# Five elementwise products per turn, on VectorE instead of GpSimd, in a two-layer retention and short-conv mixer

## The chip, the cores and the metric

The kernel runs on one core of a Trainium2 chip. The metric is the device time of one execution in microseconds (us), less is better. Three runs of the kernel before gave 1888.89, 1891.98 and 1894.93 us; their median, 1891.98, is the time before.

## What is computed

Two mixer layers over 256 tokens of width 2048, in f32. Cut to what matters here:

```python
mod = silu(c) @ w_ada + b_ada                    # shift, scale, gate
h = rmsnorm(x, norm_pre) * (1 + scale) + shift
z = h @ w_in                                     # 2048 -> 14336 columns
gb, gcin, u, g_c, q, k, v, g_r = split(z)
y_conv = gb * causal_conv3(gcin * u, conv_w)     # gcin * u: the conv gate product
y_conv = y_conv * silu(g_c)                      # gb * ...: the output gate
q, k = rope(q), rope(k) * DK ** -0.5             # t1*cos - t2*sin, t1*sin + t2*cos
y_ret = head_groupnorm(retention(q, k, v), gn_gain) * silu(g_r)
o = concat(y_conv, y_ret) @ w_out
x = x + gate * rmsnorm(o, norm_post)
```

## The kernel before, in words

**Tiling.** Activations lie transposed, channels on the 128 partitions and the 256 tokens in the free dimension. A layer is four *turns* (`TURNS`), each for two retention heads and a quarter of the conv channels. A turn goes through seven blocks of 512 weight columns in the order q/k, v, conv gate input (GC), u (UU), output gate of the conv (GB), g (GG), g_r (GR). A block is four *chunks* of 512 rows of `w_in` (1 MB each), so a turn has 28 chunks; chunk w of a turn belongs to block w // 4. After the turns come four output blocks of eight chunks of `w_out`.

**A chunk's path.** SyncE loads it into one of four slots of `stage` (L319, L338) once VectorE has released the slot. ScalarE rounds it to `w_hi` (L433, two halves), VectorE computes the rest, `w_lo = stage - w_hi` (L622, two halves), and TensorE multiplies with both: L996 to L999 for most blocks, L1016 to L1018 for the v block (24 matmuls of 512 columns per chunk, the *V chunks*). `w_hi` and `w_lo` are double-buffered by the chunk's parity. Each engine has its own instruction stream, in program order, and waits on semaphores.

**VectorE's order.** The loop at L748 goes over w = 4 to 31, one step per chunk. A step is: for chunks with an *ada chunk* before them (a piece of the adaLN matrix, 12 per turn in layer 0 and 4 in layer 1, one of them always before the second V chunk, w = 5), three multiply-accumulates into `acc` (L640 or L643, 128x512), then the two halves of `w_lo` (L622), then the fourth accumulate, then the slots' release; otherwise just `w_lo` and the release. Behind that come the works tied to a block b = w // 4 - 1, whose chunks are finished, and a position `late` = w % 4 in it: at late 0 the block's four result tiles are added up out of PSUM (L661), into bufA for q/k, UU and GG, bufB for GC and GB, `sg` for GR; the conv's three taps (L813, L815) at (UU, 2), (GB, 0) and (GB, 2); the final gate product (L826) at (GG, 2), and so on.

**ScalarE** copies the half-swapped q/k from bufA to bufB after the q/k tiles (L544, L545), between its casts.

**GpSimd's order** (L922 to L943), per turn: wait for the q/k tiles, bufC = bufA * cos (L926); wait for the swapped copies, bufB = bufB * sin (L928); bufC = bufC + bufB (L930), which releases TensorE's score matmuls behind the v block (L1088). Then four small instructions for the heads' rstd (L933 to L938). Then, when the UU tiles are there, cu = bufA * bufB (L940); after the conv's last tap bufC = bufC * bufB (L942). All five products are 128x1024 f32. The sine and cosine tables `sin_t`, `cos_t` (128x256, broadcast over four tiles) are made on GpSimd before the loops.

**Counting.** `me.then` counts VectorE's or GpSimd's own steps on a semaphore, `PER_TURN` is their number per turn, and `me.wait` waits for the last of them.

Of the kernel before, what the change touches and what calls it, by code (L numbers as in the profile page):

```python
# [79 lines left out]
LO_TURN = 24  # L80
LO_LAYER = TURNS * LO_TURN + Z_OUT

PER_TURN = [ADA_TURN[l] * GROUPS * CK + 4 + (CONV_K - 1) * TILES for l in range(LAYERS)]

PRM_B, PRM_PRE, PRM_POST, PRM_GN, PRM_C, PRM_CW = 0, 96, 128, 160, 192, 208
PRM = 304
# [16 lines left out]
def build(nc, x, c, positions, norm_pre, norm_post, w_ada, b_ada, w_in, conv_w, gn_gain, w_out,  # L103
          consts, decay, out):
    ctx = ExitStack()
    with ctx:
# [3 lines left out]
        def sem(name):  # L110
            return ctx.enter_context(nc.semaphore(name))
# [101 lines left out]
        s_tpc = sem("start_copied")  # L213
        s_cs = sem("c_silu_done")
        s_tab = sem("angle_done")
        s_xc = sem("x_copied")
        s_sin = sem("sines_done")
        s_ot = sem("out_transposed")
# [38 lines left out]
        def stage_pos(layer, j, w):  # L257

            base = ADA_START * GROUPS
            for earlier in range(layer):  # L260
                base += TURNS * (CH_TURN + ADA_TURN[earlier] * GROUPS) + CH_OUT
            return base + w + sum(ada_before(layer)[:w + 1]) + j * (CH_TURN + ADA_TURN[layer] * GROUPS)
# [11 lines left out]
        def ck(layer, j, w):  # L274

            return CH_LAYER * layer + w + j * CH_TURN
# [337 lines left out]
        def _(dve):  # L614
            me = Steps(dve, s_vd)
            V = nc.vector

            def low(slot, parity, n):

                for h in range(2):  # L620
                    dve.wait_ge(s_hi, 2 * n + h + 1)
                    V.tensor_tensor(w_lo[:, 2 * parity + h, :, :], stage[:, slot, 2 * h:2 * h + 2, :],  # L622
                                    w_hi[:, 2 * parity + h, :, :].bitcast(F32), ALU.subtract).then_inc(s_lo, 1)
# [6 lines left out]
            def split(slot, parity, n):  # L630
                low(slot, parity, n)
                used(n)
# [106 lines left out]
            for l in range(LAYERS):  # L739
# [2 lines left out]
                span = CH_TURN + ADA_TURN[l] * GROUPS  # L742
                for w in range(LEAD if l == 0 else 2, LEAD):
                    split(stage_pos(l, 0, w) % SLOTS, w % 2, ck(l, 0, w))
                with dve.Fori(0, TURNS) as j:
                    me.loop(j, PER_TURN[l])
                    seen = 0
                    for w in range(LEAD, CH_TURN + LEAD):  # L748
# [17 lines left out]
                        if late == 0 and b != VV:  # L766
                            dst = {QK: bufA, GC: bufB, UU: bufA, GB: bufB, GG: bufA, GR: sg}[b]
                            if b == GB:
                                dve.wait_ge(s_cu, TURNS * l + 1 + j)
                            for t in range(TILES):  # L770
                                z_out_of(t, zlo_at(l, j, b) + t + 1, dst[:, t, :])
                        if (b, late) == (VV, 2):
                            for h in range(2):
                                dve.wait_ge(s_sc, 2 * TURNS * l + h + 1 + 2 * j)
                                if h == 0:
                                    dve.wait_ge(s_dec, 16 * (TURNS * l + 1) + 16 * j)
                                V.tensor_tensor(p_sb[:, h, 0:S], SC[h][:, 0:S], dec[:, h, :], ALU.mult)
                                V.tensor_tensor(p_sb[:, h, S:S + P], SC[h][:, S:S + P], dec[:, h, 0:P], ALU.mult)\
                                    .then_inc(s_p, 1)
# [96 lines left out]
        @block.gpsimd  # L876
        def _(pool):
            me = Steps(pool, s_pd)
            G = nc.gpsimd

            def step(ins):
                me.then(ins)
                me.wait()

            def rstd(k):
                pool.wait_ge(s_var, k)
                G.tensor_tensor(rs2[:, :], var2[:, :], mhalf[:, 0:NT], ALU.pow).then_inc(s_pow, 1)

            step(G.memset(mhalf[:, :], -0.5))

            ang, u, n = bufC[:, 1, :], bufC[:, 2, :], bufC[:, 3, :]
            pool.wait_ge(s_pos, 16)
            pool.wait_ge(s_par, 16 * 12)
            step(G.tensor_copy(u, bufC[:, 0, :].bitcast(I32)))
            step(G.tensor_scalar(ang, u, ident[:, P:P + 1], None, ALU.mult))
            turn = 2 * math.pi
            c1 = round(turn * 2 ** 9) / 2 ** 9
            c2 = round((turn - c1) * 2 ** 21) / 2 ** 21
            c3 = turn - c1 - c2
            whole = 1.5 * 2 ** 23  # L900
            for scale in (2.0 ** 20, 2.0 ** 10, 1.0):
                step(G.tensor_scalar(n, ang, 1.0 / (turn * scale), None, ALU.mult))
                step(G.tensor_scalar(n, n, whole, None, ALU.add))
                step(G.tensor_scalar(n, n, whole, None, ALU.subtract))
                for part in (c1, c2, c3):
                    step(G.tensor_scalar(u, n, part * scale, None, ALU.mult))
                    step(G.tensor_tensor(ang, ang, u, ALU.subtract))
            edge = float(np.nextafter(np.float32(math.pi), np.float32(0)))
            step(G.tensor_scalar(ang, ang, edge, None, ALU.min))
            step(G.tensor_scalar(ang, ang, -edge, None, ALU.max))  # L910
            pool.sem_inc(s_tab, 1)
            rstd(1)
            pool.wait_ge(s_sin, 2)

            step(G.tensor_tensor(cos_t[:, :], cos_t[:, :], cos_t[:, :], ALU.mult))
            step(G.tensor_scalar(cos_t[:, :], cos_t[:, :], -2.0, 1.0, ALU.mult, ALU.add))
            step(G.tensor_scalar(sin_t[:, :], sin_t[:, :], ident[:, P + 1:P + 2], None, ALU.mult))

            def all4(t):
                return t[:, :].rearrange("p (o s) -> p o s", o=1).broadcast_to([P, 4, S])  # L920

            for l in range(LAYERS):  # L922
                with pool.Fori(0, TURNS) as j:
                    me.loop(j, 5)
                    pool.wait_ge(s_z, z_at(l, j, VV))
                    me.then(G.tensor_tensor(bufC[:, :, :], bufA[:, :, :], all4(cos_t), ALU.mult))  # L926
                    pool.wait_ge(s_swap, 2 * TURNS * l + 2 + 2 * j)
                    me.then(G.tensor_tensor(bufB[:, :, :], bufB[:, :, :], all4(sin_t), ALU.mult))  # L928
                    me.wait()
                    G.tensor_tensor(bufC[:, :, :], bufC[:, :, :], bufB[:, :, :], ALU.add).then_inc(s_rope, 1)  # L930
                    pool.wait_ge(s_mv, TURNS * l + 1 + j)
                    hold(pool, "pool")
                    me.then(G.tensor_scalar(rs4[:, :], mv[:, :, 1], EPS, None, ALU.add))  # L933
                    me.wait()
                    me.then(G.tensor_tensor(rs4[:, :], rs4[:, :], mhalf[:, :], ALU.pow))
                    me.then(G.tensor_scalar(nb4[:, :], mv[:, :, 0], -1.0, None, ALU.mult))
                    me.wait()
                    G.tensor_tensor(nb4[:, :], nb4[:, :], rs4[:, :], ALU.mult).then_inc(s_rs, 1)  # L938
                    pool.wait_ge(s_z, z_at(l, j, GB))
                    G.tensor_tensor(cu[:, :, 2:S + 2], bufA[:, :, :], bufB[:, :, :], ALU.mult).then_inc(s_cu, 1)  # L940
                    pool.wait_ge(s_cv, TURNS * l + 1 + j)
                    G.tensor_tensor(bufC[:, :, :], bufC[:, :, :], bufB[:, :, :], ALU.mult).then_inc(s_cg, 1)  # L942
                    me.end(TURNS)  # L943

                for nb in range(D // BLK - 1):
                    pool.wait_ge(s_o, KT * l + TILES * (nb + 1))
                    if nb == 0:
                        ins = G.tensor_tensor(bufB[:, 0:2, :], bufA[:, 0:2, :], bufA[:, 2:4, :], ALU.add)
                    else:
                        step(G.tensor_tensor(bufB[:, 2:4, :], bufA[:, 0:2, :], bufA[:, 2:4, :], ALU.add))  # L950
                        ins = G.tensor_tensor(bufB[:, 0:2, :], bufB[:, 0:2, :], bufB[:, 2:4, :], ALU.add)
                    ins.then_inc(s_opre, 1)
                    pool.wait_ge(s_opre, (D // BLK - 1) * l + nb + 1)
                rstd(2 * l + 2)

                last = slice(4 * POOL_G, 4 * POOL_G + 4)
                pool.wait_ge(s_ou, KT * (l + 1))
                pool.wait_ge(s_rtsb, l + 1)
                step(G.tensor_tensor(yr[:, last, :], yr[:, last, :],
                                     rt_sb.rearrange("p (o s) -> p o s", o=1).broadcast_to([P, 4, S]), ALU.mult))  # L960
                G.tensor_tensor(xT[:, last, :], yr[:, last, :], xT[:, last, :], ALU.add).then_inc(s_xp, 1)
                if l < LAYERS - 1:
                    rstd(2 * l + 3)
# [275 lines left out]
```

## Time and profile before

| | |
|---|---|
| median of 3 runs | 1891.98 us (1888.89 to 1894.93) |
| profiled execution, first to last instruction (span) | 1889.6 us |
| profiled execution, own device time | not given beside the span |
| TensorE matmul busy | 1787.6 us (95%) |
| VectorE busy | 1229.4 us (65%) |
| ScalarE busy | 811.7 us (43%) |
| GpSimd busy | 194.1 us (10%) |
| mean granted TensorE clock | 0.973 |
| HBM traffic | 217 GB/s over the span |

In all profile rows PE is TensorE's matmuls, PEld its weight loads, DVE VectorE, ACT ScalarE, POOL GpSimd; L622 is line 622 of the kernel. "Busy" is the union of the instructions' spans. Times in timelines are counted from the first instruction.

### The profile page before, as it was taken

The page shows a single profiled execution, that of the slowest core. Times are in us where ns is not written, and L with a number is a line of the kernel's source. Part 1 is how long each engine was busy: PE and PEld are TensorE (multiplying, and loading weights), DVE is VectorE, ACT ScalarE, POOL GpSimd, SP SyncE. Part 2 cuts the span into 40 slices and gives each one's busy share as a digit, 9 for nine tenths or more (in the row PEclk, how much of TensorE's full clock was granted, in tenths as well). Part 3 has the DMA queues.
Part 4 walks back from the last instruction along what each step waited for, and adds up shares of the span by engine and source line. Part 5 has one row for each costly group of instructions (what it writes and reads, how often), then busy time and mean ns, then how long its engine had stood idle before and what let it go on. Part 6 is the DMA issues. An engine that isn't in the chain of part 4 may idle for free.

```text
span 1889.6 us, 28049 instructions
## 1 busy us (share of the span) xinstructions
PE 1787.6 (95%) x9855; PEld 1510.1 (80%) x9855; DVE 1229.4 (65%) x1486; ACT 811.7 (43%) x1054; POOL 194.1 (10%) x129
## 2 busy tenths in 40 slices
PE   6779998999899899999998999899989989999997
PEld 3358887888788788888887788788878878888886
DVE  1367887786778777864547566657666765666554
ACT  2233443444344434454444344443544443445443
POOL 5010101010110101000001010101011010100001
PEclk9799999999999999999999999999999999999998
DMA  9977785678667677855552656555655646565551
GB/s 351 346 275 267 265 273 204 240 253 268 222 215 282 201 267 253 286 179 178 181 176 89 208 198 223 178 192 191 222 178 196 239 154 216 206 215 186 197 182 45
DMA packets 223250, 410.89 MB, mean 217 GB/s; under 512 B 7168, under 2 KB 40496, under 8 KB 222896
## 3 DMA queue, kind: packets, MB, share of 16 engines
q1 hardware_dynamic: 223008, 409.46, 62.5%
q8 instruction: 61, 1.00, 0.2%
q10 hardware_dynamic: 144, 0.13, 0.1%
q14 instruction: 37, 0.30, 0.0%
HBM read 407.46 MB, written 2.10 MB: 217 GB/s over the span
## 4 chain that ended last, share of the span: by engine, by line
PE 80%; DVE 11%; issue 3%; DMA 2%; ACT 1%; SPq 1%; POOL 0%; DVEq 0%; ACTq 0%; POOLq 0%
PE Z L999 43%; PE Z L997 23%; DVE acc L643 6%; DVE w_lo L622 3%; PE Z L1016 3%; PE Z L1017 3%; PE Z L1018 3%; PE Z L996 2%; DMA stage<-in_w_ada 1%; DMA yr<-in_x 1%; PE SC L1134 1%; DVE bufC L815 1%; PE SC L1051 0%; ACT lo_sb L439 0%; DMA stage<-in_w_in 0%
## 5 line engine op out<-in xcount | busy, mean ns | idle before, releaser
L999 PE MATMUL Z<-H,w_hi 128*128 128x512 f32 x3392 | 1201.6, 397 | 0.0
L997 PE MATMUL Z<-H,w_lo 128*128 128x256 f32 x3584 | 974.8, 281 | 6.2 <-DVE w_lo L622 4.7
L622 DVE TENSOR_TENSOR w_lo<-stage,w_hi 128x1024 fp32r<-128x1024 f32 x576 | 711.7, 1259 | 402.6 <-ACT w_hi L433 370.6
L433 ACT CAST w_hi<-stage 128x1024 fp32r<-128x1024 f32 x576 | 592.0, 1050 | 664.8 <-PE Z L999 470.9
L999 PEld LDWEIGHTS Z<-H,w_hi 128*128 128x128 f32 x3392 | 638.1, 188 | 144.1
L997 PEld LDWEIGHTS Z<-H,w_lo 128*128 128x128 f32 x3584 | 677.4, 189 | 33.9 <-DVE w_lo L622 12.2
L643 DVE SCALAR_TENSOR_TENSOR acc<-stage,c_silu,acc 128x512 f32<-128x512 f32 x240 | 244.4, 1018 | 7.4 <-DVE w_lo L622 2.1
L999 PE MATMUL Z<-Y,w_hi 128*128 128x512 f32 x480 | 169.5, 396 | 0.0
L439 ACT COPY lo_sb<-Z 128x256 f32<-128x256 f32 x224 | 82.0, 372 | 182.3 <-PE Z L999 147.6
L1016 PE MATMUL Z<-w_hi,H 128*128 128x512 f32 x256 | 109.2, 427 | 38.7 <-DVE w_lo L622 38.2
L997 PE MATMUL Z<-Y,w_lo 128*128 128x256 f32 x512 | 137.6, 279 | 0.0
L1017 PE MATMUL Z<-w_lo,H 128*128 128x512 f32 x256 | 106.6, 416 | 0.0
L1018 PE MATMUL Z<-w_hi,H 128*128 128x512 f32 x256 | 106.3, 415 | 0.0
L999 PEld LDWEIGHTS Z<-Y,w_hi 128*128 128x128 f32 x480 | 90.1, 188 | 20.3
L997 PEld LDWEIGHTS Z<-Y,w_lo 128*128 128x128 f32 x512 | 96.4, 188 | 2.8
L1016 PEld LDWEIGHTS Z<-w_hi,H 128*128 128x128 f32 x256 | 52.9, 207 | 54.1 <-DVE w_lo L622 41.5
L996 PE MATMUL Z<-H,w_hi 128*128 128x512 f32 x192 | 80.7, 420 | 2.0 <-DVE H L698 1.9
L926 POOL TENSOR_TENSOR bufC<-bufA,cos_t 128x1024 f32<-128x1024 f32 x8 | 20.6, 2581 | 441.2 <-DVE bufA L661 441.2
L661 DVE TENSOR_TENSOR bufA<-Z,lo_sb 128x256 f32<-128x256 f32 x96 | 39.4, 423 | 39.1 <-ACT lo_sb L439 32.0
L1017 PEld LDWEIGHTS Z<-w_lo,H 128*128 128x128 f32 x256 | 53.0, 207 | 11.1
L1018 PEld LDWEIGHTS Z<-w_hi,H 128*128 128x128 f32 x256 | 52.2, 204 | 11.9
L446 ACT CAST acc_hi<-acc 128x512 fp32r<-128x512 f32 x24 | 14.9, 620 | 97.0 <-DVEq L761 51.2
(147 smaller groups left out, 922.0 us busy)
## 6 DMA issues: line engine op xcount, KB each, us to landing
stage<-in_w_in SPq DMA_DIRECT2D x192, 1024.0 KB, 5.3
stage<-in_w_ada SPq DMA_DIRECT2D x96, 1024.0 KB, 7.2
stage<-in_w_out SPq DMA_DIRECT2D x64, 1024.0 KB, 5.1
stage<-in_w_in SPq DMA_DIRECT2D x64, 512.0 KB, 5.9
dec<-decay SPq DMA_DIRECT2D x9, 256.0 KB, 5.1
yr<-in_x SPq DMA_DIRECT2D x2, 1024.0 KB, 11.4
out<-stage SPq DMA_DIRECT2D x8, 256.0 KB, 2.5
bufC<-in_positions ACTq DMA_DIRECT2D x1, 128.0 KB, 5.5
```

Source lines behind the costliest of these rows:

```text
L433: nc.scalar.copy(w_hi[:, 2 * parity + h, :, :], stage[:, slot, 2 * h:2 * h + 2, :]).then_inc(s_hi, 1)
L439: nc.scalar.copy(lo_sb[:, t % 2, :], Z[t][:, S:2 * S]).then_inc(s_zlo, 1)
L622: V.tensor_tensor(w_lo[:, 2 * parity + h, :, :], stage[:, slot, 2 * h:2 * h + 2, :], w_hi[:, 2 * parity + h, :, :].bitcast(F32), ALU.subtr ...
L643: ins = V.scalar_tensor_tensor(acc[:, :], w, c_silu[:, k:k + 1], acc[:, :], ALU.mult, ALU.add)
L661: V.tensor_tensor(dst, Z[t][:, 0:S], lo_sb[:, t % 2, :], ALU.add).then_inc(s_z, 1)
L926: me.then(G.tensor_tensor(bufC[:, :, :], bufA[:, :, :], all4(cos_t), ALU.mult))
L996: T.matmul(Z[t][:, :], wh, act, start=True, stop=False)
L997: ins = T.matmul(Z[t][:, 0:S], wl, act[:, 0:S], start=False, stop=False)
L999: ins = T.matmul(Z[t][:, :], wh, act, start=False, stop=stop)
L1016: T.matmul(Z[i][:, :], hh, wh, start=kc == 0 and a == 0, stop=False)
L1017: T.matmul(Z[i][:, :], hh, wl, start=False, stop=False)
L1018: ins = T.matmul(Z[i][:, :], hl, wh, start=False, stop=kc == GROUPS - 1 and a == CK - 1)
```

## The change

The five products leave GpSimd's stream and take places in VectorE's: the cos product right behind the q/k tiles (at w = 4), the sin product and the sum at the end of the next step (w = 5), the conv gate product behind the UU tiles (w = 16), the output-gate product at the end of the step (GB, 3), w = 23. GpSimd keeps the tables and the heads' rstd, and signals once that the tables are ready.

```diff
--- before.py
+++ after.py
@@ -80,7 +80,7 @@
 LO_TURN = 24
 LO_LAYER = TURNS * LO_TURN + Z_OUT
 
-PER_TURN = [ADA_TURN[l] * GROUPS * CK + 4 + (CONV_K - 1) * TILES for l in range(LAYERS)]
+PER_TURN = [ADA_TURN[l] * GROUPS * CK + 4 + 2 + (CONV_K - 1) * TILES for l in range(LAYERS)]
 
 PRM_B, PRM_PRE, PRM_POST, PRM_GN, PRM_C, PRM_CW = 0, 96, 128, 160, 192, 208
 PRM = 304
@@ -213,6 +213,7 @@
         s_tpc = sem("start_copied")
         s_cs = sem("c_silu_done")
         s_tab = sem("angle_done")
+        s_tables = sem("sines_scaled")
         s_xc = sem("x_copied")
         s_sin = sem("sines_done")
         s_ot = sem("out_transposed")
@@ -614,6 +615,9 @@
         def _(dve):
             me = Steps(dve, s_vd)
             V = nc.vector
+
+            def all4(t):
+                return t[:, :].rearrange("p (o s) -> p o s", o=1).broadcast_to([P, 4, S])
 
             def low(slot, parity, n):
 
@@ -742,6 +746,8 @@
                 span = CH_TURN + ADA_TURN[l] * GROUPS
                 for w in range(LEAD if l == 0 else 2, LEAD):
                     split(stage_pos(l, 0, w) % SLOTS, w % 2, ck(l, 0, w))
+                if l == 0:
+                    dve.wait_ge(s_tables, 1)
                 with dve.Fori(0, TURNS) as j:
                     me.loop(j, PER_TURN[l])
                     seen = 0
@@ -769,6 +775,22 @@
                                 dve.wait_ge(s_cu, TURNS * l + 1 + j)
                             for t in range(TILES):
                                 z_out_of(t, zlo_at(l, j, b) + t + 1, dst[:, t, :])
+                            if b == QK:
+
+                                dve.wait_ge(s_z, z_at(l, j, VV))
+                                me.then(V.tensor_tensor(bufC[:, :, :], bufA[:, :, :], all4(cos_t), ALU.mult))
+                            if b == UU:
+                                dve.wait_ge(s_z, z_at(l, j, GB))
+                                V.tensor_tensor(cu[:, :, 2:S + 2], bufA[:, :, :], bufB[:, :, :], ALU.mult)\
+                                    .then_inc(s_cu, 1)
+                        if (b, late) == (QK, 1):
+                            dve.wait_ge(s_swap, 2 * TURNS * l + 2 + 2 * j)
+                            me.then(V.tensor_tensor(bufB[:, :, :], bufB[:, :, :], all4(sin_t), ALU.mult))
+                            me.wait()
+                            V.tensor_tensor(bufC[:, :, :], bufC[:, :, :], bufB[:, :, :], ALU.add).then_inc(s_rope, 1)
+                        if (b, late) == (GB, 3):
+                            dve.wait_ge(s_cv, TURNS * l + 1 + j)
+                            V.tensor_tensor(bufC[:, :, :], bufC[:, :, :], bufB[:, :, :], ALU.mult).then_inc(s_cg, 1)
                         if (b, late) == (VV, 2):
                             for h in range(2):
                                 dve.wait_ge(s_sc, 2 * TURNS * l + h + 1 + 2 * j)
@@ -915,19 +937,11 @@
             step(G.tensor_tensor(cos_t[:, :], cos_t[:, :], cos_t[:, :], ALU.mult))
             step(G.tensor_scalar(cos_t[:, :], cos_t[:, :], -2.0, 1.0, ALU.mult, ALU.add))
             step(G.tensor_scalar(sin_t[:, :], sin_t[:, :], ident[:, P + 1:P + 2], None, ALU.mult))
-
-            def all4(t):
-                return t[:, :].rearrange("p (o s) -> p o s", o=1).broadcast_to([P, 4, S])
+            pool.sem_inc(s_tables, 1)
 
             for l in range(LAYERS):
                 with pool.Fori(0, TURNS) as j:
-                    me.loop(j, 5)
-                    pool.wait_ge(s_z, z_at(l, j, VV))
-                    me.then(G.tensor_tensor(bufC[:, :, :], bufA[:, :, :], all4(cos_t), ALU.mult))
-                    pool.wait_ge(s_swap, 2 * TURNS * l + 2 + 2 * j)
-                    me.then(G.tensor_tensor(bufB[:, :, :], bufB[:, :, :], all4(sin_t), ALU.mult))
-                    me.wait()
-                    G.tensor_tensor(bufC[:, :, :], bufC[:, :, :], bufB[:, :, :], ALU.add).then_inc(s_rope, 1)
+                    me.loop(j, 3)
                     pool.wait_ge(s_mv, TURNS * l + 1 + j)
                     hold(pool, "pool")
                     me.then(G.tensor_scalar(rs4[:, :], mv[:, :, 1], EPS, None, ALU.add))
@@ -936,10 +950,6 @@
                     me.then(G.tensor_scalar(nb4[:, :], mv[:, :, 0], -1.0, None, ALU.mult))
                     me.wait()
                     G.tensor_tensor(nb4[:, :], nb4[:, :], rs4[:, :], ALU.mult).then_inc(s_rs, 1)
-                    pool.wait_ge(s_z, z_at(l, j, GB))
-                    G.tensor_tensor(cu[:, :, 2:S + 2], bufA[:, :, :], bufB[:, :, :], ALU.mult).then_inc(s_cu, 1)
-                    pool.wait_ge(s_cv, TURNS * l + 1 + j)
-                    G.tensor_tensor(bufC[:, :, :], bufC[:, :, :], bufB[:, :, :], ALU.mult).then_inc(s_cg, 1)
                     me.end(TURNS)
 
                 for nb in range(D // BLK - 1):
```

## Rows read from the trace of the kernel before

**Rows 1.** The page: busy us and share by engine; GB/s in 40 slices of the span.
```profile
PE 1787.6 (95%) x9855; PEld 1510.1 (80%) x9855; DVE 1229.4 (65%) x1486; ACT 811.7 (43%) x1054; POOL 194.1 (10%) x129
...
GB/s 351 346 275 267 265 273 204 240 253 268 222 215 282 201 267 253 286 179 178 181 176 89 208 198 223 178 192 191 222 178 196 239 154 216 206 215 186 197 182 45
```

**Rows 2.** Waits of engine PE: who waited for whom, total us, times, longest us.
```profile
PE Z L1016 <- DVE w_lo L622: 38.2, 8, 4.8
...
PE Z L997 <- DVE w_lo L622: 4.7, 16, 0.9
```

**Rows 3.** Timeline of DVE, 300 to 324 us: start, us, instruction, idle before.
```profile
300.66 1.62 DVE L661 TENSOR_TENSOR bufA<-Z,lo_sb 128x256 f32<-128x256 f32 x4 [0.24 <-DVE w_lo L622]
302.19 0.48 DVE L640 TENSOR_SCALAR acc<-stage,c_silu 128x512 f32<-128x512 f32 x1
302.70 5.58 DVE L643 SCALAR_TENSOR_TENSOR acc<-stage,c_silu,acc 128x512 f32<-128x512 f32 x2
308.44 4.26 DVE L622 TENSOR_TENSOR w_lo<-stage,w_hi 128x1024 fp32r<-128x1024 f32 x2 [0.16 <-ACT w_hi L433]
312.63 0.74 DVE L643 SCALAR_TENSOR_TENSOR acc<-stage,c_silu,acc 128x512 f32<-128x512 f32 x1
313.65 2.36 DVE L622 TENSOR_TENSOR w_lo<-stage,w_hi 128x1024 fp32r<-128x1024 f32 x2 [0.28 <-DVE acc L643]
316.30 2.33 DVE L643 SCALAR_TENSOR_TENSOR acc<-stage,c_silu,acc 128x512 f32<-128x512 f32 x3 [0.29 <-DVE w_lo L622]
```

**Rows 4.** Timeline of POOL, 300 to 425 us.
```profile
302.35 2.59 POOL L926 TENSOR_TENSOR bufC<-bufA,cos_t 128x1024 f32<-128x1024 f32 x1 [56.39 <-DVE bufA L661]
304.89 2.85 POOL L928 TENSOR_TENSOR bufB<-bufB,sin_t 128x1024 f32<-128x1024 f32 x1
307.82 2.67 POOL L930 TENSOR_TENSOR bufC<-bufC,bufB 128x1024 f32<-128x1024 f32 x1
...
381.80 2.84 POOL L940 TENSOR_TENSOR cu<-bufA,bufB 128x1024 f32<-128x1024 f32 x1 [9.89 <-DVE bufA L661]
417.00 2.85 POOL L942 TENSOR_TENSOR bufC<-bufC,bufB 128x1024 f32<-128x1024 f32 x1 [32.36 <-DVE bufC L815]
```

**Rows 5.** Timeline of DVE, 377 to 390 and 414 to 428 us.
```profile
381.63 4.34 DVE L643 SCALAR_TENSOR_TENSOR acc<-stage,c_silu,acc 128x512 f32<-128x512 f32 x3
...
416.83 4.35 DVE L643 SCALAR_TENSOR_TENSOR acc<-stage,c_silu,acc 128x512 f32<-128x512 f32 x3
```

**Rows 6.** Timeline of PE, near 92, 306 to 312, near 422 us.
```profile
92.20 0.39 PE L997 MATMUL Z<-H,w_lo 128*128 128x256 f32 x1 [0.85 <-DVE w_lo L622]
...
306.33 0.39 PE L1017 MATMUL Z<-w_lo,H 128*128 128x512 f32 x1
306.55 0.39 PE L1018 MATMUL Z<-w_hi,H 128*128 128x512 f32 x1
311.62 0.80 PE L1016 MATMUL Z<-w_hi,H 128*128 128x512 f32 x1 [4.68 <-DVE w_lo L622]
...
422.61 0.39 PE L997 MATMUL Z<-H,w_lo 128*128 128x256 f32 x1 [0.54 <-DVE w_lo L622]
422.83 0.40 PE L999 MATMUL Z<-H,w_hi 128*128 128x512 f32 x1
```

**Rows 7.** Timeline of ACT, 300 to 324 us.
```profile
304.46 3.89 ACT L433 CAST w_hi<-stage 128x1024 fp32r<-128x1024 f32 x4
318.91 2.13 ACT L433 CAST w_hi<-stage 128x1024 fp32r<-128x1024 f32 x2 [10.56 <-DMA stage<-in_w_in]
```

**Rows 8.** Timeline of PE, 311.6 to 316.5 us.
```profile
313.07 0.63 PE L1016 MATMUL Z<-w_hi,H 128*128 128x512 f32 x1
313.50 0.63 PE L1017 MATMUL Z<-w_lo,H 128*128 128x512 f32 x1
```

**Rows 9.** Sums by stretch: two turns; then slow stretches after the eight waits, PE alone.
```profile
core 0: us, PE busy (x) PEld busy (x) DVE busy (x) ACT busy (x) POOL busy (x), PEclk, DMA share, GB/s
301.20:475.10 173.90, 168.17 (x917) 144.28 (x917) 133.77 (x165) 74.94 (x95) 17.02 (x9) 0.98 0.70 244
1202.10:1372.10 170.00, 165.00 (x901) 142.13 (x900) 110.33 (x128) 74.43 (x92) 17.18 (x9) 0.98 0.58 199
...
core 0: us, PE busy (x), PEclk, DMA share, GB/s
311.61:317.20 5.59, 5.58 (x13) 0.50 0.43 124
sum 39.94, PE 39.85; mean PE 4.98
```

**Rows 10.** Groups of DVE by line and form: xcount, busy us, mean ns, idle us.
```profile
L826 DVE TENSOR_TENSOR bufC<-bufC,bufA 128x1024 f32<-128x1024 f32 x8 | 9.8, 1225 | 1.8 <-DVE w_lo L622 1.8
...
L860 DVE TENSOR_TENSOR yr<-yr,IN 128x512 f32<-128x512 f32 x12 | 8.2, 679 | 2.1 <-PE IN L1038 2.1
```

## The prediction

> **What bounds the kernel now.** I read the page's busy times first, then who waits for whom, then one turn of layer 0 instruction by instruction. TensorE's matmuls are busy 95% of the span, VectorE 65%, GpSimd 10% [rows 1]. So VectorE and GpSimd work matters only where TensorE waits for it. The list of TensorE's waits gives that place [rows 2]: 38.2 us in 8 waits of up to 4.8 us, one per turn, all for `w_lo`, in front of L1016, the first matmul of a V chunk. A second row has 4.7 us in 16 short waits for `w_lo`.
>
> The timeline of VectorE around such a wait (turn 1 of layer 0, counted from 0) shows what makes it late [rows 3]. After the last q/k tile (bufA, ended at 302.28) the next chunk's ada accumulation starts: L640 and then two L643 that take 5.58 us together. Three of the same L643 take 2.33 us at 316.30, some 0.79 us from start to start. The following two L622 take 4.26 us; undisturbed, at 313.65, two take 2.36. So three instructions are stretched by about 2.0, 2.0 and 1.9 us. GpSimd's timeline has exactly three instructions there, the rotary ones, from 302.35 to 310.49 [rows 4], and each stretched VectorE instruction ends about half a microsecond or a microsecond after the GpSimd instruction beside it. The same happens at the two other places: three L643 take 4.34 us beside the GpSimd product at 381.80, and 4.35 beside the one at 417.00 [rows 4, 5]. It is not a slowdown in proportion: VectorE stands still while GpSimd runs, for about 2.0 us of each of the five GpSimd products, 10.0 us a turn. The Trainium skill states this as a rule (SBUF — State Buffer, Who interferes with whom): a VectorE instruction with two SBUF inputs is fully blocked by a GpSimd instruction that reads SBUF. The trace agrees, 2.8 us against 0.75.
>
> TensorE issued its last matmul of the first V chunk at 306.55 and the next at 311.62, after 4.68 us of idleness [rows 6]. ScalarE wasn't to blame: its casts for the next two chunks run from 304.46 to 308.35, the first half ready at about 305.5 [rows 7]. And then TensorE pays a second time: its granted clock falls to 0.50, the 1.2 GHz level, and matmuls follow each other at 0.43 us [rows 8] instead of 0.225 [rows 6]. The stretches at half clock after the eight waits sum to 39.94 us [rows 9].
>
> **What is removed.** Five GpSimd products per turn, eight turns. Nobody waits for GpSimd's result there except through VectorE's delay.
> (a) The wait in front of the second V chunk: 38.2 us [rows 2].
> (b) The half-clock stretch behind it. Of its time, 1 - 0.225/0.43 = 0.477 is lost: 39.94 x 0.477 = 19.0 us, gone if the idle time that precedes each fall goes.
> (c) The short waits, mostly in the chunks behind the other two products; one of 0.54 us stands at 422.61, right after the stretched L643 [rows 5, 6]. The longest, of 0.9 us, stands before the turns, at 92.20; the other 3.8 us go.
> Sum 61.0 us.
>
> **What is added.** Five VectorE products of 128x1024 f32 per turn. The row nearest to them, L826, the same operation and shape with SBUF operands, takes 1225 ns [rows 10]; a successor that needs no result of it starts 1.14 us later (two L622 in 2.36, [rows 3]). That is about 6.1 us of VectorE per turn, against 10.0 of standing still: VectorE gains 3.9 us a turn. The broadcast table operand has no row of its own with both inputs in SBUF; L860, with a broadcast PSUM operand, takes 679 ns for 512 elements, and that is little over half of L826 [rows 10]. So from below the broadcast costs nothing extra, and from above I allow twice the time, 2.45 us, for two of the five (about what GpSimd takes for the same product, [rows 4]). I take 1.225, the nearest row.
>
> What counts is where they stand. In the same turn:
> - cos product: the q/k tiles end at 302.28, 0.15 for the semaphore, start 302.4, successor at 303.55.
> - ada front: 0.51 + 0.79 + 0.75 = 2.05, to 305.6; plus 0.15, then `w_lo` of the second chunk from 305.75 to 306.97. TensorE could start at 306.94 (311.62 - 4.68). **New wait about 0.1 us** in place of 4.68. TensorE starts at about 307.05.
> - second half of `w_lo` to 308.1, last ada part to 308.8, the semaphore for the slot to 309.05; sin product to 310.3; it waits for that, and the add runs from 310.45, successor at 311.6. `w_lo` of the third V chunk's first half ends at 312.8. TensorE's 24 matmuls at 0.225 end at 312.45. **New wait about 0.4 us.**
> - third chunk from 312.9 to 318.3. VectorE: second half to 313.95, 0.3, ada front 2.33, 0.15, first half of the fourth chunk's `w_lo` to 317.95, 0.35 us ahead of need. Its load landed at 318.91, which was 5.5 us after the ada part that freed the slot (312.63 + 0.74) [rows 3, 7]; now that part ends at 308.8, so it lands at about 314.3 and isn't late.
> In turn 0 the casts and tiles lie 0.3 us less favourably. So new waits are 8 x 0.5 + 0.3 = 4.3 us. Both steps are present in layer 1, whose turn has its ada chunk in the same place; wherever VectorE's queue has no slack at these points, every later `w_lo` waits behind the products.
> - conv gate product: 1.2 us in front of an ada front that no longer loses 2.0: `w_lo` comes 0.8 us earlier. The output-gate product stands behind its chunk's `w_lo`, which comes 2.0 us earlier, and the next one's 0.7 earlier. Both cost nothing: the stretch that they remove is larger than they are.
> - the wait for the sine tables: those are finished long before the first turn, nothing. No DMA is moved; SyncE's loads follow VectorE's release of slots, as above.
>
> **Sum.** 61.0 - 4.3 = 56.7 us off. The page gives the span, 1889.6, and no other time of the profiled execution; the median of the runs, 1891.98, lies 2.4 above it. Span 1833, median 1891.98 - 56.7 = 1835.3; I say **1836**.
>
> **Load against standing still.** VectorE is the busier engine by far: 133.8 us of a 173.9 us turn, GpSimd 17.0 [rows 9]. Taken as plain load, the move puts 6.1 us on it in each turn, 49 us in all; taken as above, it takes 3.9 us a turn away. The stretches decide for me; the other reading is rival 3. The Trainium skill speaks for that reading (Perfetto Trace Analysis, Optimizing Scalar/DVE Operations): with VectorE saturated, work may be moved to ScalarE or even GpSimd, the opposite of this change; by it alone the sum would be up to 49 us more, 1941. The same section warns that the two share a read port.
>
> **Rivals.**
> 1. *The clock falls anyway* (0.08). The new waits of 0.1 and 0.4 us still bring the half clock, so (b) stays: 1835.3 + 19.0 = 1854. Against it: no slow stretch follows the 0.54 us wait at 422.61, whose successor matmuls keep their pace.
> 2. *The loads become the bound in layer 0* (0.07). Its turns move 244 GB/s at a DMA share of 0.70 [rows 9], against 199 in layer 1. If the ring of four slots can't go faster, its four turns gain nothing, 4 x 56.7 / 8 = 28 us less: 1864. Against it: the same engines move 351 GB/s in the page's first slice [rows 1], and the long wait for a load, 10.56 us [rows 7], comes from a slot freed late by the stretched chain.
> 3. *Slower: VectorE is the bound* (0.03). If something else in that place stretches VectorE, say ScalarE's half-swap copies or the loads, the products are plain added load: the cos product is added in front of a `w_lo` that already decides the path, and the conv product in front of one without slack. That is 2 x 1.2 us a turn, 8 turns: +19 us, 1911, and at most the 49 us above. It decides as soon as the stretches survive GpSimd's leaving. Against it: at 381.80 and 417.00 there are no swap copies, and the stretch has the same size.
> 4. *No change* (0.02): something behind `w_lo` holds the second chunk to the same moment. Nothing in rows 6 and 7 does: about 1892.
>
> **Numbers.** The forecast has 0.80, with its own range of 1829 to 1846: below, no new waits at all (1831) and a little from VectorE's queue running ahead elsewhere; above, products at twice the time for the two with a table (2 x 1.2 x 8 / 2 = 10 us, half of it behind slack). The 80% range reaches to rival 1: 1828 to 1856. A measurement of this kernel can tell about 0.3%, 5.7 us, from no change. Faster by more than that 0.95, within it 0.02, slower 0.03.
>
> **What would show it.** In the changed profile L643 should take 0.75 us everywhere in the turns, POOL's busy time should fall from 194 to about 84 us, VectorE's from 1229 to some 1198 (8 x 3.9 less). The wait of L1016 for `w_lo` should fall from 38.2 us to under 1, a new one of about 0.4 us should stand before the third V chunk, and the granted clock should stay at 1.0 through the turns; turns of 166.5 us in layer 0 and 163 in layer 1. I am wrong if L643 stays at 2.8 us beside nothing on GpSimd, if the third V chunk waits over 1 us, or if the half clock comes back without a wait.

## The result and the profile after

Four runs of the changed kernel took 1822.24 to 1828.59 us, median 1824.43; the kernel before, in four runs beside them, 1893.45. The ratio is 0.9642, 95% interval 0.9624 to 0.966: faster by 69 us where 56.7 were forecast (by 67.6 us, if counted from the 1891.98 that the forecast starts from). 1824.4 lies below the stated range, which began at 1828. The profiled execution took 1823.35 us, its span is 1821.5.

The page of the changed kernel: busy times, GpSimd's and TensorE's granted clock in 40 slices, and the queue that carries instructions.

```profile
PE 1756.4 (96%) x9855; PEld 1493.1 (82%) x9855; DVE 1194.6 (66%) x1526; ACT 813.3 (45%) x1054; POOL 84.2 (5%) x89
...
POOL 5000000000000000000010000000000000000001
PEclk9899999999999999999999999999999999999998
...
q14 instruction: 52, 0.43, 0.1%
```

GpSimd's busy time fell from 194.1 to 84.2 us and VectorE's from 1229.4 to 1194.6 [rows 1], as forecast (84 and 1198). The waits of TensorE, against [rows 2]:

```profile
PE Z L1026 <- DVE bufA L665: 5.9, 5, 1.9
...
PE Z L1007 <- DVE w_lo L626: 0.4, 1, 0.4
PE Z L1026 <- DVE w_lo L626: 0.2, 1, 0.2
```

L1026 is the L1016 of before. Its 38.2 us behind `w_lo` are 0.2 us, and the 16 short waits one of 0.4. In their place stands a wait for the q/k tiles (bufA), 5.9 us in five, that the prediction doesn't have. VectorE's timeline at the place of [rows 3] (the same turn, 11 us earlier):

```profile
291.31 1.23 DVE L781 TENSOR_TENSOR bufC<-bufA,cos_t 128x1024 f32<-128x1024 f32 x1
292.45 0.48 DVE L644 TENSOR_SCALAR acc<-stage,c_silu 128x512 f32<-128x512 f32 x1
292.97 1.54 DVE L647 SCALAR_TENSOR_TENSOR acc<-stage,c_silu,acc 128x512 f32<-128x512 f32 x2
294.66 2.36 DVE L626 TENSOR_TENSOR w_lo<-stage,w_hi 128x1024 fp32r<-128x1024 f32 x2 [0.16 <-DVE acc L647]
...
297.94 1.22 DVE L788 TENSOR_TENSOR bufB<-bufB,sin_t 128x1024 f32<-128x1024 f32 x1 [0.26 <-DVE acc L647]
299.20 1.22 DVE L790 TENSOR_TENSOR bufC<-bufC,bufB 128x1024 f32<-128x1024 f32 x1
300.34 2.35 DVE L626 TENSOR_TENSOR w_lo<-stage,w_hi 128x1024 fp32r<-128x1024 f32 x2
```

The two L643 of 5.58 us (L647 now) take 1.54, the two `w_lo` 2.36, and all five products 1.22 to 1.23 us. TensorE's timeline at both new places of waiting:

```profile
295.32 0.39 PE L1027 MATMUL Z<-w_lo,H 128*128 128x512 f32 x1
295.55 0.39 PE L1028 MATMUL Z<-w_hi,H 128*128 128x512 f32 x1
295.95 0.50 PE L1026 MATMUL Z<-w_hi,H 128*128 128x512 f32 x1
...
301.07 0.39 PE L1027 MATMUL Z<-w_lo,H 128*128 128x512 f32 x1
301.29 0.39 PE L1028 MATMUL Z<-w_hi,H 128*128 128x512 f32 x1
301.62 0.50 PE L1026 MATMUL Z<-w_hi,H 128*128 128x512 f32 x1
```

Matmuls follow each other after 0.225 us; before the second V chunk it is 0.40, before the third 0.33. So the new waits are 0.17 and 0.1 us, too short for a row that shows idleness. The clock is full there; the sums by stretch for the two turns of [rows 9] are

```profile
core 0: us, PE busy (x) PEld busy (x) DVE busy (x) ACT busy (x) POOL busy (x), PEclk, DMA share, GB/s
290.20:454.90 164.70, 164.67 (x914) 142.25 (x915) 129.00 (x168) 74.88 (x94) 3.28 (x4) 1.00 0.74 258
1153.10:1316.90 163.80, 161.88 (x900) 139.76 (x901) 105.86 (x134) 74.64 (x93) 3.46 (x4) 1.00 0.61 207
```

The turn in layer 0 takes 164.7 us, 1.8 less than I said; the one in layer 1 163.8, 0.8 more than I said, with a new loss at its end.

**Where the 68.1 us between the spans come from**, read from the start of the first matmul of each of the 288 chunks in the two traces (a step is the change of the difference from one chunk to the next; the rows sum to 67.9 by rounding):

| place | forecast, us gained | found, us gained |
|---|---|---|
| wait before the second V chunk | 38.2, less 0.9 new | 36.0 |
| half clock behind it, less the third V chunk's wait | 19.0 - 3.4 | 16.8 |
| waits behind the conv gate product (w = 17) | part of 3.8 | 2.6 |
| waits behind the output-gate product (w = 23, 24) | part of 3.8 | 6.0 |
| all other chunks of turns and output blocks | 0 | 7.6 |
| wait for the q/k tiles at a turn's start (w = 4) | 0 | -5.7 |
| the opening, before the turns | 0 | 2.3 |
| between the layers, and the end | 0 | 2.3 |

The rotary place came out at 52.8 us against 52.9. The error is in the other rows. The opening's 2.3 us seem to belong to the one execution of before that was profiled: in every other profile here, those made from the kernel before among them, the fourth chunk starts 1.1 to 2.7 us earlier than in it. Of the 2.3 us between the layers, 1.6 is a half-clock stretch at the head of layer 1 that four of the twelve profiles have (before, e6, e8 and e9) and the others don't; it comes and goes without the change.

### The profile page after: what moved, and what is told of

The parts are those of the page before. It is cut to its first block, busy times and chain, and to the rows that moved or that the text cites. A ratio compares the mean times of both kernels' runs of the same rounds, so it can differ in the third digit from the quotient of the medians.

```text
span 1821.5 us, 28042 instructions
## 1 busy us (share of the span) xinstructions
PE 1756.4 (96%) x9855; PEld 1493.1 (82%) x9855; DVE 1194.6 (66%) x1526; ACT 813.3 (45%) x1054; POOL 84.2 (5%) x89
## 4 chain that ended last, share of the span: by engine, by line
PE 89%; DVE 3%; issue 3%; DMA 2%; ACT 1%; SPq 1%; POOL 0%; DVEq 0%; ACTq 0%; POOLq 0%
PE Z L1009 47%; PE Z L1007 25%; PE Z L1026 3%; PE Z L1027 3%; PE Z L1028 3%; PE Z L1006 3%; DMA stage<-in_w_ada 1%; DVE w_lo L626 1%; DMA yr<-in_x 1%; PE SC L1144 1%; DMA stage<-in_w_in 0%; PE SC L1061 0%; ACT w_hi L434 0%; PE IN L1041 0%; PE SC L1119 0%
## 5 line engine op out<-in xcount | busy, mean ns | idle before, releaser
L626 DVE TENSOR_TENSOR w_lo<-stage,w_hi 128x1024 fp32r<-128x1024 f32 x576 | 695.2, 1232 | 372.8 <-ACT w_hi L434 324.2
L647 DVE SCALAR_TENSOR_TENSOR acc<-stage,c_silu,acc 128x512 f32<-128x512 f32 x240 | 179.6, 748 | 7.4 <-DVE w_lo L626 2.1
L1026 PE MATMUL Z<-w_hi,H 128*128 128x512 f32 x256 | 102.5, 401 | 6.3 <-DVE bufA L665 5.9
L1028 PE MATMUL Z<-w_hi,H 128*128 128x512 f32 x256 | 100.5, 393 | 0.0
L1027 PE MATMUL Z<-w_lo,H 128*128 128x512 f32 x256 | 100.5, 392 | 0.0
L1026 PEld LDWEIGHTS Z<-w_hi,H 128*128 128x128 f32 x256 | 48.4, 189 | 23.0 <-DVE w_lo L626 12.6
L947 POOL TENSOR_SCALAR rs<-mv 128x4 f32<-128x4 f32 x8 | 6.1, 766 | 1183.2 <-DVE mv L811 1183.2
L1028 PEld LDWEIGHTS Z<-w_hi,H 128*128 128x128 f32 x256 | 48.5, 189 | 10.5
L1027 PEld LDWEIGHTS Z<-w_lo,H 128*128 128x128 f32 x256 | 48.4, 189 | 9.6
## 6 DMA issues: line engine op xcount, KB each, us to landing
yr<-in_x SPq DMA_DIRECT2D x2, 1024.0 KB, 11.4
```

Of the source, the lines that this page charges most:

```text
L647: ins = V.scalar_tensor_tensor(acc[:, :], w, c_silu[:, k:k + 1], acc[:, :], ALU.mult, ALU.add)
L1026: T.matmul(Z[i][:, :], hh, wh, start=kc == 0 and a == 0, stop=False)
L1027: T.matmul(Z[i][:, :], hh, wl, start=False, stop=False)
L1028: ins = T.matmul(Z[i][:, :], hl, wh, start=False, stop=kc == GROUPS - 1 and a == CK - 1)
```

## The experiments

**Two theories for the rows that weren't forecast.** *Code fetch*: VectorE's loop in layer 1 has become too long to stay in its instruction memory. *Pace*: TensorE runs its matmul pairs in one of two rhythms, and what it waits for on the way decides which. And for the whole gain: *blocking* by GpSimd, against *plain load*.

**e1, the loop's end announced.** The changed kernel with

```diff
-                with dve.Fori(0, TURNS) as j:
+                with nc.Fori(0, TURNS, engines=(dve.engine,), hint_back_edge=True) as j:
```

> The changed kernel, with the branch at the end of VectorE's turn loops announced at the top of each iteration. Theory (code fetch): in layer 1 the longer loop no longer stays in VectorE's instruction memory, and each of the three returns to its head costs VectorE 5.4 to 5.9 us of idleness, of which 1.9, 2.1 and 1.5 us reach TensorE, once with a half-clock stretch of 3.4 us behind it. With the announcement the idleness of 'issue' shrinks in both layers and TensorE gets back about 5.5 + 1.6 = 7 us: some 1817 us against 1824. Rival (the gap is semaphore or register work at the loop's head): the gaps of about 5 us stay, 1824 us.

1817.12 us, ratio 0.9597 (0.9579 to 0.9614): 7 us less than the change. In the changed kernel VectorE stands idle at the head of each later turn of layer 1, and TensorE behind it (its timeline, then TensorE's):

```profile
1143.31 0.88 DVE L822 SCALAR_TENSOR_TENSOR yr<-SC,prm,sg 128x256 f32 x2 [0.71 <-DVE w_lo L626]
1149.95 2.36 DVE L626 TENSOR_TENSOR w_lo<-stage,w_hi 128x1024 fp32r<-128x1024 f32 x2 [5.76 <-issue]
...
1150.95 0.40 PE L1009 MATMUL Z<-H,w_hi 128*128 128x512 f32 x1
1153.11 0.49 PE L1026 MATMUL Z<-w_hi,H 128*128 128x512 f32 x1 [1.76 <-DVE bufA L665]
```

In the kernel before layer 1 had no such gap and layer 0 three, 4.6 to 4.8 us each, behind which TensorE's waits for bufA sum to 0.4 us; the idleness by "issue" before `w_lo` went from 14.2 us in three to 31.2 in six. With the announcement no such row is left. The instruction queue of e1's page:

```profile
q14 instruction: 22, 0.18, 0.0%
```

22 packets, against 52 with the change and 37 before: 15 more for three returns in layer 1, and 30 less for six. The place w = 4 gives 1.2 us instead of -5.7. Code fetch holds: the packets, the idleness and TensorE's loss go together. The Trainium skill (Advanced Engine Details and Errata, ISA Cache) has a cache of two lines of 256 instructions for engines other than TensorE. The traces don't contradict it, but don't show it either: in them a turn of layer 1 has 299 records of VectorE in e3, which returns without the fetch, and 301 in e2 and 304 in the changed kernel, which fetch; all are more than one such line and less than two. Whether the loop's length or its position against the lines decides, no run here tells.

**e2 and e3, one half of the change each.** e2 leaves the gate products on GpSimd, e3 the rotary ones:

```diff
-                            if b == UU:
...
-                                V.tensor_tensor(cu[:, :, 2:S + 2], bufA[:, :, :], bufB[:, :, :], ALU.mult)\
...
+                    G.tensor_tensor(cu[:, :, 2:S + 2], bufA[:, :, :], bufB[:, :, :], ALU.mult).then_inc(s_cu, 1)
...
```

> Only the three rotary products are on VectorE; the conv gate and output-gate products stay on GpSimd. Blocking theory: this is where nearly all of the gain is, the 4.7 us wait before the second V chunk and the half clock behind it, 36 + 18 = 54 us: about 1839 us against 1893 before, L643's twins still stretched to 2.8 us at the two conv places. If the code-fetch theory holds, three instructions decide whether layer 1 pays at its loop's return: with the fetch 1839, without it some 6 us less. Rival (the gain comes from all five in equal parts): 0.6 of 69, about 1852.

> Only the conv gate and output-gate products are on VectorE; the rotary products stay on GpSimd. Blocking theory: the short waits behind the two places go, 0.3 + 0.6 to 1.1 us a turn, 5 to 8 us in all; the 4.8 us wait per turn and its half clock stay: about 1886 us. Rival (equal parts): 0.4 of 69, about 1866. Two added products may or may not push layer 1's loop out of the instruction memory: the 'issue' idleness before w_lo at the loop's head shows it.

e2: 1842.69 us, ratio 0.9746 (0.9722 to 0.9771), 3.7 above the 1839 expected with the fetch. e3: 1870.51, ratio 0.988 (0.9857 to 0.9902), 22 us where 5 to 8 were expected. Spans fell by 49.3 and 20.2 us, together 69.5 for the change's 68.1. Of the rows of the table, e2 has the second V chunk (36.1) and the half clock (16.8), 0.3 at w = 23 and 24, and nothing in the output blocks; e3 has 2.6 at w = 17, 5.8 at w = 23 and 24, and 7.5 in the other chunks. So it's the gate products' leaving that brings the unforeseen gain. The sum of the two halves fits better than it should: the opening's 1.7 and 2.5 us stand in both, and e3 has 3.4 us from shorter half-clock stretches behind the V chunk's wait, though that wait is the old one (38.1 us in eight). Why they were shorter in e3's profile stays open. The instruction queues of e2 and of e3:

```profile
q14 instruction: 52, 0.43, 0.1%
```

```profile
q14 instruction: 38, 0.30, 0.0%
```

With the three rotary products more the loop fetches, with the two gate products more it doesn't: the limit lies between.

**e4, the load without the unblocking.** The kernel before with

```diff
+                        for _ in range({(QK, 0): 1, (QK, 1): 2, (UU, 0): 1, (GB, 3): 1}.get((b, late), 0)):
...
+                            me.then(V.tensor_tensor(sg[:, :, :], bufA[:, :, :], bufA[:, :, :], ALU.mult))
```

> The kernel before, GpSimd's five products untouched, with five more VectorE products (bufA * bufA into sg, which is free there) at the places where the change puts them: the load without the unblocking. The output stays that of the reference. Plain-load rival of the prediction: 1.2 us before the second V chunk and 1.2 behind UU are not covered, 19 us, and with layer 1's loop longer also its fetch, 5 us: 1912 to 1917 us. If VectorE's added work is hidden everywhere: 1893. Blocking theory: GpSimd's products still stretch VectorE as before, and the wait before the second V chunk grows from 4.8 to about 6 us.

1912.34 us, ratio 1.0113 (1.0088 to 1.0138). The waits of its TensorE:

```profile
PE Z L1021 <- DVE w_lo L622: 49.1, 8, 6.3
PE Z L1002 <- DVE w_lo L622: 15.9, 17, 1.6
```

49.1 instead of 38.2 us, and 15.9 instead of 4.7: both places that rival 3 named. The time is its price (1911), but partly by luck. By the starts of the chunks the two places cost 11.4 and 11.2 us, and two that it didn't name 3.6 (w = 24) and 2.1 (w = 4; VectorE's idleness by "issue" is 29.0 us in six here too). Some 9 us come back elsewhere, 4.2 of them because the turns' and output blocks' other chunks go at the fast pace more often, the rest in the opening and between the layers.

**e5 and e6, GpSimd beside VectorE.** The changed kernel; GpSimd waits for the q/k tiles and then makes three products that nobody needs, or eight memsets:

```diff
+                    pool.wait_ge(s_z, z_at(l, j, VV))
+                    for _ in range(3):
+                        me.then(G.tensor_tensor(sg[:, :, :], bufA[:, :, :], bufA[:, :, :], ALU.mult))
+                        me.wait()
```

```diff
+                    for n in range(8):
+                        me.then(G.tensor_tensor(sg[:, 3, 0:4], mhalf[:, :], mhalf[:, :], ALU.mult))
+                        me.then(G.memset(sg[:, 0:3, :], 0.0))
+                        me.wait()
```

> The changed kernel, with three products put back on GpSimd beside the q/k tiles' end that nobody waits for (sg = bufA * bufA, both free for it there). VectorE keeps the five products. Blocking theory: each of the three holds VectorE for about 2.0 us (L647 at 2.8 instead of 0.75 us, or a product at 3.2 instead of 1.2), 6 us before the third V chunk: the wait before the second V chunk comes back with about 4 us and the half clock behind it, 8 x (4 + 2.3) = 50 us: about 1875 us. Rival (dependence on the rotary results or ScalarE's copies made VectorE late, not GpSimd's access): 1824 us, L647 at 0.75 us.

> As the run before it, but GpSimd does eight memsets (128x768, into sg) there, with a four-element product ahead of each: it writes SBUF for as long or longer, and reads almost none. If the standstill comes from GpSimd reading SBUF beside a VectorE instruction with two SBUF inputs, nothing is stretched: L647 at 0.75 us, 1824 us. If any GpSimd access to SBUF blocks VectorE, L647 is stretched by a memset's length and the wait before the second V chunk comes back: 1850 us or more.

e5: 1877.29 us, 0.9909 (0.9889 to 0.993). e6: 1830.07, 0.9667 (0.9648 to 0.9686). GpSimd's and VectorE's timelines in e5:

```profile
298.49 7.27 POOL L947 TENSOR_TENSOR sg<-bufA 128x1024 f32<-128x1024 f32 x3 [102.49 <-DVE bufA L665]
...
298.44 1.23 DVE L781 TENSOR_TENSOR bufC<-bufA,cos_t 128x1024 f32<-128x1024 f32 x1
299.59 2.12 DVE L644 TENSOR_SCALAR acc<-stage,c_silu 128x512 f32<-128x512 f32 x1
301.74 4.56 DVE L647 SCALAR_TENSOR_TENSOR acc<-stage,c_silu,acc 128x512 f32<-128x512 f32 x2
306.46 2.36 DVE L626 TENSOR_TENSOR w_lo<-stage,w_hi 128x1024 fp32r<-128x1024 f32 x2 [0.15 <-DVE acc L647]
```

Three products that have nothing to do with VectorE's work bring the wait back, 37.6 us in its row. Blocking is shown. In e6:

```profile
293.36 0.74 POOL L948 MEMSET sg<- 128x768 f32 x1
294.36 0.74 POOL L948 MEMSET sg<- 128x768 f32 x1
...
292.13 1.23 DVE L781 TENSOR_TENSOR bufC<-bufA,cos_t 128x1024 f32<-128x1024 f32 x1
293.28 1.09 DVE L644 TENSOR_SCALAR acc<-stage,c_silu 128x512 f32<-128x512 f32 x1
294.41 1.54 DVE L647 SCALAR_TENSOR_TENSOR acc<-stage,c_silu,acc 128x512 f32<-128x512 f32 x2
296.10 2.36 DVE L626 TENSOR_TENSOR w_lo<-stage,w_hi 128x1024 fp32r<-128x1024 f32 x2 [0.16 <-DVE acc L647]
```

The memsets run beside two L647 and two `w_lo`, all unstretched. Only L644 is stretched, from 0.48 to 1.09 us: it is a `tensor_scalar`, one SBUF input, and the memset from 293.36 falls on it. That is about 0.6 us of VectorE in each turn; by the starts of the chunks it costs TensorE 4.3 us at the second V chunk in the eight turns, of the 6.4 us between the two spans. My expectation had no such case, but the Trainium skill does (SBUF — State Buffer, Who interferes with whom): an instruction with two SBUF inputs is blocked by GpSimd's reads alone, while `tensor_scalar` may use both port pairs and then collides with writes too. Both halves agree with the trace.

**e7, the products placed later.** e1 with cos and sin product behind `w_lo` of the second V chunk, the sum behind the third's:

```diff
-                            if b == QK:
...
                         if (b, late) == (QK, 1):
+                            dve.wait_ge(s_z, z_at(l, j, VV))
+                            me.then(V.tensor_tensor(bufC[:, :, :], bufA[:, :, :], all4(cos_t), ALU.mult))
...
+                        if (b, late) == (QK, 2):
+                            me.wait()
```

> The version with the announced branch, and the rotary products placed later: cos and sin product behind w_lo of the second V chunk, the sum behind w_lo of the third. VectorE's work up to the fourth chunk is the same. From the traces, TensorE's issue before the second V chunk is 0.17 us late and before the third 0.1 us. Theory: the second chunk's lateness goes (8 x 0.17 = 1.4 us), the third's stays as it is, the fourth chunk's slack of 0.5 us in turn 0 to 3 us is untouched: 1815.7 against 1817.1. Rival (the third chunk now waits by more than the second gains, since both products and not one stand right before it): 1817 to 1820.

1818.24 us (0.959 to 0.9625 of before): no difference to e1. The second chunk gains 0.12 us a turn and the third 0.09, but in layer 0 the fourth comes 0.6 us late, since the sum now stands right before it; neither the theory nor its rival had named the fourth:

```profile
305.81 0.39 PE L1027 MATMUL Z<-w_hi,H 128*128 128x512 f32 x1
306.65 0.50 PE L1025 MATMUL Z<-w_hi,H 128*128 128x512 f32 x1 [0.46 <-DVE w_lo L626]
```

**e8, a nudge.** The kernel before, and one matmul more:

```diff
+                    if nb == 0:
+                        T.matmul(IN[0][:, 0:P], ones[:, :], ones[:, :], start=True, stop=True)
```

> The kernel before, with one more 128x128 matmul on TensorE (into a PSUM bank that is free) ahead of each layer's output blocks. In the profiles, a chunk of 32 matmuls without any wait takes 5.42 us (first to last start) or 5.31, in long unbroken runs of one kind: in the kernel before, layer 0's 32 output chunks go at 5.42, layer 1's at 5.31. Theory (the pace is a rhythm into which TensorE falls after a disturbance, and that lasts until the next): the nudge can change it, and 32 chunks then change from one to the other together, 3.4 us. Rival (the pace belongs to the place in the program or to what the other engines do then): layer 0's output chunks stay at 5.42 and layer 1's at 5.31.

A single run: 1885.3 us, span 1883.5. Matmuls begun or running in 140 us within layer 0's output blocks (window view of TensorE alone: us, busy and number, clock, DMA), in the kernel before, in the changed one, and in e8:

```profile
830.00:970.00 140.00, 140.00 (x795) 1.00 0.54 185
```

```profile
790.00:930.00 140.00, 140.00 (x809) 1.00 0.57 191
```

```profile
830.00:970.00 140.00, 140.00 (x809) 1.00 0.57 190
```

795, 809 and 809, with no wait and the full clock in each. One small matmul changed the pace of 32 chunks: 3.1 us, less 0.2 for the matmul. The time of a single run shows nothing by itself; 1.9 of the 6.1 us between the spans lie in the opening and 1.2 in half-clock stretches. That the pace isn't the execution's chance is seen where it is carried on: in the twelve profiles there are 96 borders between a turn and the next turn or the output blocks, and in 95 of them the chunks behind the border's first go at the pace of the last chunk before it, slow or fast. The one exception is the nudged border of layer 0 in e8. In e8's layer 1 the pace was the fast one, and the nudge left it. Where the rhythm shows is in the spacing of the pairs. Slow (before), and fast (changed kernel):

```profile
850.13 0.28 PE L997 MATMUL Z<-Y,w_lo 128*128 128x256 f32 x1
850.25 0.40 PE L999 MATMUL Z<-Y,w_hi 128*128 128x512 f32 x1
850.48 0.28 PE L997 MATMUL Z<-Y,w_lo 128*128 128x256 f32 x1
...
851.19 0.28 PE L997 MATMUL Z<-Y,w_lo 128*128 128x256 f32 x1
```

```profile
785.08 0.40 PE L1009 MATMUL Z<-H,w_hi 128*128 128x512 f32 x1
785.31 0.28 PE L1007 MATMUL Z<-H,w_lo 128*128 128x256 f32 x1
785.43 0.39 PE L1009 MATMUL Z<-H,w_hi 128*128 128x512 f32 x1
...
786.12 0.39 PE L1009 MATMUL Z<-H,w_hi 128*128 128x512 f32 x1
```

Three pairs take 1.06 us (850.13 to 851.19, the second pair begun at 850.48) against 1.04 (785.08 to 786.12). Of the chunks of turns and output blocks that aren't the first of their block and have no wait, 118 go at 5.42 us in the kernel before and 51 in the changed one; 67 x 0.107 is 7.2 us, nearly the table's 7.6.

**e9 and e10, a nudge where the slow rhythm always stands.** e1 with one more matmul ahead of the GC block, of 128 columns (e9) or of 32 (e10, shown):

```diff
+                    if b == GC:
+                        T.matmul(IN[0][:, 0:32], ones[:, :], ones[:, 0:32], start=True, stop=True)
```

> The version with the announced branch, and one more 128x128 matmul on TensorE ahead of each turn's GC block, into a PSUM bank that is free. In all kernels so far the seven chunks behind the first of GC go at the slow pace, 5.42 us, until the first of GB. If the pace is a rhythm that a nudge changes, as it did in front of the output blocks, they go at 5.31: 8 turns x 7 chunks x 0.107 = 6.0 us less, minus the nudge itself, 8 x 0.2 to 0.4 us: 1813 to 1815 against 1817.1. If the nudge leads back to the same rhythm: 1819 to 1820.

> The same with a matmul of 32 columns in place of 128: a smaller disturbance, so perhaps another rhythm behind it. Fast pace: 1812 to 1814. Slow pace: 1818 to 1819.

e9: 1820.46 us, 0.9614 (0.9601 to 0.9628); no chunk of GC or UU changes its pace. The expectation had overlooked that in layer 1 the UU chunks behind the block's first go at 5.31 in every kernel, so that 36 chunks were to be won and not 56, 3.9 us and not 6.0. e10: 1814.94, 0.9586 (0.9572 to 0.96). In all eight turns the GC and UU chunks behind their block's first go at 5.31 in it (in one such stretch 238 matmuls in 41 us against 235 in e1), which gains 2.7 us against e1 with the eight nudges paid. But layer 0's output blocks are back at the slow pace, 796 matmuls in 140 us, which takes 3.2 us away. e10 is the fastest median of the study, yet its interval overlaps e1's; I would keep e1 and count e10 as luck.

## Why the prediction was wrong, point by point

The steps that failed are term (c), the short waits, which was mis-sized, and the gate products' leaving, whose further gain the sum put at nothing. Together they brought 16.2 us (8.6 and 7.6) where 3.8 were forecast. A loss that was left out, 5.7 us at the turns' start, hides part of it.

- **Blocking, and the wait before the second V chunk**: the mechanism was right. e5 shows the cause, e2 the size. That the two rows agree to 0.1 us is luck, since three misses cancel. The new waits were put at 4.3 us and are 0.17 + 0.1 a turn, 2.2 us. The half clock, term (b), was put at 19.0 us and is about 17.3 (in e1, where none comes back: 16.5 by the chunks' starts, and 0.8 for the third chunks' new waits). And one of the eight half-clock stretches came back, 3.4 us long, behind one of the waits for the q/k tiles that were not foreseen.
- **Term (c), the short waits, 3.8 us**: found 8.6 (2.6 + 6.0). The row counts idleness, and matmuls overlap. Behind the conv gate product, in the kernel before:

```profile
386.82 0.40 PE L999 MATMUL Z<-H,w_hi 128*128 128x512 f32 x1
387.39 0.38 PE L997 MATMUL Z<-H,w_lo 128*128 128x256 f32 x1 [0.17 <-DVE w_lo L622]
```

TensorE starts 0.57 us after the last matmul instead of 0.23, and the row has 0.17. Each short wait costs about 0.17 us more than its row, 2.5 us for the fifteen in the turns. The remaining 2.3 us or so lie in these same chunks, some of which change from one rhythm to the other; that part is read from the steps and not tested by itself.
- **"Both cost nothing", the gate products**: right that they cost nothing, wrong that removing them is worth only (c). With the waits behind them gone, TensorE goes at the fast rhythm for more of the chunks, 7.6 us. Nothing in the rows that I read would have shown it; the start times of the chunks did, 5.42 against 5.31, and I hadn't laid them side by side.
- **What is queued behind VectorE's loop**: left out. Five more products with their waits in layer 1's loop cost a code fetch at each return, 5.5 us of TensorE there. The three idle stretches by "issue" in layer 0 were in the trace before.
- **The range** reached 7 us below the forecast, with "no new waits at all" as its lower end. It took the size of every removed wait as read, and had no term for a gain that no row names.
- **Rival 1** (the clock falls anyway): no. **Rival 2** (the loads): no, layer 0's turn moves 258 GB/s against 244. **Rival 3**: its condition is false; its price came out in e4 (1912), in part by luck. **Rival 4**: no.

## What to carry to other kernels

Before elementwise work is put on GpSimd to relieve VectorE, look whether VectorE's two-input instructions beside it are longer than elsewhere: here each GpSimd product of 2.6 to 2.85 us took 2.0 us from VectorE, more than the 1.2 us that VectorE needs for the same product. Charge added instructions in a loop with the code fetch at its return, and look for idleness by "issue" at the loop's head. And take the cost of a wait from the spacing of the matmuls' starts, not from the idle time.

## What wasn't expected of the hardware

- TensorE runs the same stream of matmul pairs at 353 or at 347 ns a pair (5.42 or 5.31 us a chunk) with no wait and at the full clock, for 32 chunks on end and more; one small matmul more can change from one to the other (e8, e10), and sometimes doesn't (e9), and the change of pace goes with the removal of waits in e3. What decides it stays open.
- Returning to the head of its loop in layer 1 (304 records a turn in the trace) cost VectorE 5.4 to 5.9 us, of which 1.5 to 2.1 us reached TensorE; the three rotary products more in the loop brought it (e2), the two gate products didn't (e3), and announcing the branch took it away in both layers.
- A GpSimd memset of 0.74 us delayed a `tensor_scalar` beside it by 0.6 us and left two-input instructions alone (e6).
- A wait of 1.9 us between the layers was followed by a half-clock stretch in the profile of before and by none in that of the changed kernel, though the wait was the same. Of the twelve profiles four have it; what decides stays open.
